# Spacer tensors that shift matmul operands by 32 or 96 bytes in one decoder layer

## What is computed

```python
for l in range(DEPTH):
    mix = hybrid_mixer(x, w_in[l], b_in[l], pool_w[l], ...)   # pooling, RG-LRU and short-conv branches, gates
    x = layer_norm(ALPHA * x + mix, ln_g[l, 0], ln_b[l, 0])
    xa = memory_cross_attention(x, mem, xa_w_q[l], xa_w_k[l], xa_w_v[l], xa_w_o[l])   # 4 heads, 256 memory tokens
    x = layer_norm(ALPHA * x + xa, ln_g[l, 1], ln_b[l, 1])
    ff = swiglu(x, ffn_w_gate[l], ffn_w_up[l], ffn_w_down[l])   # 1024 -> 2816 -> 1024
    x = layer_norm(ALPHA * x + ff, ln_g[l, 2], ln_b[l, 2])
```

## Time and profile before

| | |
|---|---|
| median of 3 executions | 1027.07 us (1026.95 to 1035.94) |
| the profiled execution's own time | 1027.04 us |
| its span, first to last instruction | 1025.3 us |
| TensorE busy | 1012.6 us (99%), 5740 matmuls |
| TensorE weight loads busy | 888.3 us (87%) |
| VectorE, ScalarE, GpSimd busy | 620.1, 442.9, 42.4 us |
| DMA | 110.88 MB, mean 108 GB/s |

### The profile page before, as it was taken

The page is one execution under the profiler, slowest core; times in us unless marked ns, Lnnn a source line. Parts: engine busy times, 40 slices in busy tenths (PEclk is TensorE's granted clock), DMA queues, the critical chain, the costliest instruction groups (busy, mean ns, idle before and its releaser), DMA issues.

```text
span 1025.3 us, 14409 instructions
## 1 busy us (share of the span) xinstructions
PE 1012.6 (99%) x5740; PEld 888.3 (87%) x5740; DVE 620.1 (60%) x818; ACT 442.9 (43%) x599; POOL 42.4 (4%) x36
## 2 busy tenths in 40 slices
PE   8999999999999999999999999999999999999997
PEld 8888888888888888888888998889999999988886
DVE  5768485876633333326585555488888888743336
ACT  5454646445422222223354434265654554532232
POOL 1000000000000000000040000040000000000000
PEclk9999999999999999999999999999999999999999
DMA  6324234132622323325253323204442432333212
GB/s 208 115 78 136 83 97 128 56 98 80 196 83 87 119 82 92 113 82 207 81 183 111 118 86 121 80 24 139 126 127 83 124 124 83 124 123 110 95 41 82
DMA packets 89040, 110.88 MB, mean 108 GB/s; under 512 B 2444, under 2 KB 81440, under 8 KB 88992
## 3 DMA queue, kind: packets, MB, share of 16 engines
q1 hardware_dynamic: 87024, 103.82, 31.9%
q0 software_dynamic: 1824, 6.32, 1.8%
q10 hardware_dynamic: 144, 0.05, 0.0%
HBM read 108.09 MB, written 2.10 MB: 107 GB/s over the span
## 4 chain that ended last, share of the span: by engine, by line
PE 95%; DVE 2%; ACT 1%; DMA 1%; POOL 0%; issue 0%; SPq 0%; DVEq 0%
PE ps L602 32%; PE ps L604 31%; PE ps L603 31%; DMA act<-in_x 1%; PE ps L631 1%; DVE xnat L1472 1%; DVE xT_l L1422 0%; ACT ps L1084 0%; PE ps L837 0%; POOL wl L565 0%; DVE probs L1463 0%; ACT wh L1042 0%; DVE wl L1414 0%; DVE xnat L1453 0%; ACT xa L1056 0%
## 5 line engine op out<-in xcount | busy, mean ns | idle before, releaser
L1414 DVE TENSOR_TENSOR wl<-raw,wh 128x1024 fp32r<-128x1024 f32 (+1 forms) x146 | 173.5, 1194 | 273.2 <-ACT wh L1042 271.7
L1042 ACT ACTIVATE wh<-raw 128x1024 fp32r<-128x1024 f32 x152 | 156.2, 1036 | 324.6 <-PE ps L604 304.0
L602 PE MATMUL ps<-xT_h,wh 128*128 128x512 f32 (+1 forms) x592 | 227.6, 384 | 1.3 <-DVE xT_l L1422 1.3
L604 PE MATMUL ps<-xT_h,wl 128*128 128x512 f32 (+1 forms) x592 | 226.9, 383 | 0.0
L603 PE MATMUL ps<-xT_l,wh 128*128 128x512 f32 (+1 forms) x592 | 226.9, 383 | 0.0
L602 PEld LDWEIGHTS ps<-xT_h,wh 128*128 128x128 f32 x592 | 111.3, 188 | 23.5 <-DVE xT_l L1422 1.5
L604 PEld LDWEIGHTS ps<-xT_h,wl 128*128 128x128 f32 x592 | 111.3, 188 | 21.8
L603 PEld LDWEIGHTS ps<-xT_l,wh 128*128 128x128 f32 x592 | 111.3, 188 | 21.7
L602 PE MATMUL ps<-wh,st_h 128*128 128x512 f32 x304 | 118.8, 391 | 0.0
L603 PE MATMUL ps<-wl,st_h 128*128 128x512 f32 x304 | 118.3, 389 | 0.0
L604 PE MATMUL ps<-wh,st_l 128*128 128x512 f32 x304 | 118.3, 389 | 0.0
(11 more groups left out here) (261 smaller groups left out, 1673.1 us busy)
## 6 DMA issues: line engine op xcount, KB each, us to landing
raw<-in_w_in SPq DMA_DIRECT2D x31, 1024.0 KB, 5.7
raw<-in_ffn_w_down SPq DMA_DIRECT2D x11, 1024.0 KB, 4.9
raw<-in_ffn_w_gate SPq DMA_DIRECT2D x20, 512.0 KB, 4.4
gb<-in_ffn_w_up SPq DMA_DIRECT2D x10, 512.0 KB, 4.2
raw<-in_ffn_w_up SPq DMA_DIRECT2D x10, 512.0 KB, 4.3
raw<-in_lru_w_out SPq DMA_DIRECT2D x4, 1024.0 KB, 5.0
raw<-in_sconv_w_out SPq DMA_DIRECT2D x4, 1024.0 KB, 5.8
raw<-in_w_mix_out SPq DMA_DIRECT2D x4, 1024.0 KB, 4.7
```

Of the source, the lines that this page charges most:

```text
L602: nc.tensor.matmul(dst, st, mv_, start=start, stop=False, skip_group_check=shared)
L604: return nc.tensor.matmul(dst, st_lo_part, mv_, start=False, stop=stop, skip_group_check=shared)
L1042: nc.scalar.activation(wh[:, ring(phase, s), 0:size], src, ACT.Copy).then_inc(w_hi.sem, 1)
L1414: nc.vector.tensor_tensor(wl[:, slot, 0:size], src, wh[:, slot, 0:size].bitcast(F32), ALU.subtract).then_inc(w_lo.sem, 1)
```

## The change

Six spacers are added, and three old ones grow, so that some operands start off a multiple of 256 bytes. No instruction is added, removed or moved: on every engine the same instructions stand in the same order, with other SBUF addresses.

```diff
--- before.py
+++ after.py
@@ -136,24 +136,28 @@
 
 
         with ExitStack() as scope:
+            sb("to_lru", [P, 8], F32, scope)
             lru_h = sb("lru_h", [P, KT, SEQ], F32R, scope)
             lru_l = sb("lru_l", [P, KT, SEQ], F32R, scope)
+            sb("to_cnv", [P, 16], F32, scope)
             cnv_h = sb("cnv_h", [P, KT, SEQ], F32R, scope)
             cnv_l = sb("cnv_l", [P, KT, SEQ], F32R, scope)
         with ExitStack() as scope:
 
 
-            sb("lru_first", [P, KT - 2, SEQ], F32, scope)
+            sb("lru_first", [P, (KT - 2) * SEQ + 8], F32, scope)
             u1 = sb("u1", [P, POOL_PAD + SEQ], F32, scope)
-            sb("to_cnv_h", [P, (2 * KT + KT - 2) * SEQ - (KT - 2) * SEQ - (POOL_PAD + SEQ)], F32, scope)
+            sb("to_cnv_h", [P, (2 * KT + KT - 2) * SEQ - (KT - 2) * SEQ - (POOL_PAD + SEQ) + 16], F32, scope)
             ra1 = sb("ra1", [P, 2, SEQ], F32, scope)
             sb("cnv_first", [P, KT - 2, SEQ], F32, scope)
             si1 = sb("si1", [P, 2, SEQ], F32, scope)
 
         with ExitStack() as scope:
             s1, s4, s2, s3 = (sb(name, [P, 1024], F32, scope) for name in ("s1", "s4", "s2", "s3"))
+        sb("to_st", [P, 8])
         st_h = sb("st_h", [P, SPLIT_SLOTS, SEQ], F32R)
         st_l = sb("st_l", [P, SPLIT_SLOTS, SEQ], F32R)
+        sb("past_st", [P, 56])
         gb = sb("gb", [P, 2, D])
         xnat = sb("xnat", [P, TT, D])
         with ExitStack() as scope:
@@ -172,8 +176,10 @@
         scaled = probs[:].rearrange("p t m -> p (t m)")
 
         with ExitStack() as scope:
+            sb("to_p", [P, 56], F32, scope)
             p_h = sb("p_h", [P, 2, SEQ], F32R, scope)
             p_l = sb("p_l", [P, 2, SEQ], F32R, scope)
+            sb("to_vr", [P, 48], F32, scope)
             vr_h = sb("vr_h", [P, 2, SEQ], F32R, scope)
             vr_l = sb("vr_l", [P, 2, SEQ], F32R, scope)
             u = (sb("u", [P, POOL_PAD + SEQ], F32, scope)[:], u1[:])
@@ -192,6 +198,7 @@
             memT_h = sb("memT_h", [P, KT, M], F32R, scope)
             memT_l = sb("memT_l", [P, KT, M], F32R, scope)
             mem_nat = sb("mem_nat", [P, MT, D], F32, scope)
+            sb("to_pT", [P, 40], F32, scope)
             pT_h = sb("pT_h", [P, MT, SEQ], F32R, scope)
             pT_l = sb("pT_l", [P, MT, SEQ], F32R, scope)
         with ExitStack() as scope:
@@ -202,7 +209,7 @@
             x12 = sb("x12", [P, 2, 4, 256], F32R, scope)
             xf = sb("xf", [P, 5, 4, 256], F32, scope)
         hidden = sb("hidden", [P, HT, SEQ])
-        sb("past_ig", [P, 32])
+        sb("past_ig", [P, 136])
         cur = sb("cur", [P, DECAY_EXP + 1, 2])
         soft = sb("soft", [P, 8, KT])
```

## The result

The changed kernel takes 1036.5 us (median of 18 executions) against 1027.01 us for the kernel before (18 executions on the same chips): 9.5 us more, a ratio of 1.0089 with a 95% interval of 1.0067 to 1.011. I had forecast 1017.8 us. What happened is the rival named "slower" in the form "settle one step higher", whose price was 1036.6 us.

The account below looks back on a forecast made before the run. TensorE, busy for 1012.6 of 1025.3 us, was taken as the bound. 1027.04 us less 9.60 (one 6.67 ns step on 1440 matmuls) plus 0.23 and 0.1 not reaching the end gave 1017.8 us; range 1011.5 to 1028.5 us.

Parts of the forecast that it names:

- the rival named "slower": Touched matmuls: shifted pairs don't settle, or settle higher; 1033.3 us at 231 ns, 1036.6 us at 233.3 ns; chance 0.11.
- settle one step higher: 1440 touched matmuls at 233.3 ns distance instead of 226.7: 9.6 us more, 1036.6 us; within a case of chance 0.11.
- What bounds the kernel: Whole kernel: TensorE busy 1012.6 of 1025.3 us, so time is matmul count times distance, plus a few small waits.
- N/2.4 plus a fixed overhead at difference 0: Matmuls with both operands on 0: 13.4 ns beyond 512 columns, 13.3 beyond 256, so overhead belongs to matmul, not column.
- Plus a second step where both operands stand at the same place: Each matmul pays another 6.67 ns if its operands coincide within 256 bytes; shifting 1440 touched ones saves 9.60 us.
- The row of 387 ns: A 512-column record behind a pause, a distance of 224 ns, taken to show that 226.7 ns is no floor.
- The first products of F: F's products on `xa`, 256 columns, displaced: 117.7 ns for some 2.8 us, called unsettled, 4.5 ns above the settled 113.2.
- The rival "more than one step": Touched matmuls: new shifts collide less than 192 does; at 215.8 ns, 15.2 us off, 1011.8 us; chance 0.14.
- The one-side rival: Shift helps only the moving operand (528 matmuls, 1023.5 us) or only the stationary one (912, 1021.3 us); chance 0.09.
- The rival "nothing": Touched 512-column matmuls stay at 226.7 ns, overhead perhaps one sixteenth of the columns; time stays 1027.0 us; chance 0.24.
- Cover and scratch tensors: Around the LayerNorms 0.23 and about 0.1 us of the saving is lost; moved scratch tensors on VectorE cost 0.
- Ports that never wait: TensorE's two independent SBUF read ports, by the skill: PE never waits, shifts are worth nothing, time stays 1027.0 us.

Follow-up runs that it names:

- the bare streams: Kernels without the layer, streaming only float32r matmuls at various operand starts and widths; 512 columns with equal starts settled at 226.7 ns, 32 bytes apart at 233.3 ns.

## Why the prediction was wrong, step by step

- **What bounds the kernel: right.** The sum over matmul distances is the time. 1440 matmuls moved by 6.4 to 6.7 ns each moved the kernel by 9.5 us; no wait appeared, and `xT`, `memT` and F kept their records as foreseen.
- **N/2.4 plus a fixed overhead at difference 0: right for four of five widths.** 320 and 384 columns, which no row of before had, came out at 146.7 and 173.3 ns, to the decimal. 448 did not (206.7 for 200.0), so it is no law.
- **"Plus a second step where both operands stand at the same place": this is the step that failed.** I had one displaced placement at one width, F's, and read its 113.2 ns as one step of a law without a width in it. F's shift does give F its 6.7 ns (11.9 us in the whole, with the shift taken away), but the same shift of 192 bytes at 512 columns costs 6.7 ns. The size was right, the sign was not, and the size by luck: the shifts used here are 32, 96, 160 and 224 bytes, and those cost 6.6 to 7.6 ns in the bare streams, where 64 bytes cost 2.2. Three numbers that fit a law are weak evidence where only one of them, at one width, carries the term in question.
- **The row of 387 ns: read for too much.** It showed that one 512-column matmul can pass in 224 ns. It didn't show that a stream can. In the bare streams single records of 388 ns do occur, at a start of 64 bytes, but in a cycle with 392 and 394, and the mean distance is 229. What had to be forecast was the mean of a settled stream.
- **The first products of F: a warning that I used only for the lower bound.** I called their 117.7 ns in the earlier trace rows unsettled. The bare streams show that it is a settled state of its own: it held to the end of groups of 48 and 72 matmuls, with the same addresses as the 113.3. That one placement has two paces in one trace already says that a shift doesn't fix the pace.
- **The slower rival: right in kind and price, too small in its chance.** "At 233.3 ns: 1440 x 6.67 = 9.6 us more, 1036.6 us" against 1036.5 measured. That its price fits so closely is again a matter of the shifts used. It got 0.11, because "F's products then do settle at 113.2 ns" was held against it, which again carried 256 columns over to 512. It should have had about as much as the forecast. The range ended at 1028.5 us and left this case out, although and the earlier trace rows showed slower paces at both widths.
- **The rival "more than one step": refuted where it was tried.** No stream of 512 columns settled below 226.7 ns at any start, pause or side. Its bound of 215.8 ns was weak from the outset: it set the 109 ns of a transpose beside 106.7, the time of 256 columns, but a transpose moves 128, and no row says how long those stream.
- **The one-side rival: the sides are alike.** The bare streams mirror each other, and in the layer the 528 moving-side and the 912 stationary-side matmuls cost nearly the same each (6.7 and 6.4 to 6.5 ns).
- **The rival "nothing", with its overhead of one sixteenth of the columns: refuted** by 320 and 384 columns.
- **Cover and scratch tensors: right as far as can be seen.** I had 0.3 of the 9.6 us not arriving. In the traces 9.2 us arrive between the first product and the last, and 9.5 by the medians, which is too close to tell. From the last `st` matmul to the end it is 7.0 us before and after, as foreseen. VectorE's total is 619.8 us against 620.1.
- **Ports that never wait** (the Trainium skill, SBUF — State Buffer, section "Who interferes with whom"): as the prediction said, the trace didn't agree for 256 columns, and it doesn't for 512 either: 389 against 395 ns with nothing but the start of one operand changed.

What stays open is the cause beneath the distances: why a shift helps at one width and hurts at another, and why 448 columns have the largest overhead at difference 0. The runs give the distances by start, width and entry; no run looks at the memory itself. The records of the weight loads (PEld) narrow it a little. Moving operand at 0, then at 32 with 512 columns:

```profile
L120 PEld LDWEIGHTS ps<-m_zero_h,w_h x24: 187/188/330, 22.3 to 39.6; 128*128 128x128 f32 x24
...
L124 PEld LDWEIGHTS ps<-m_thirtytwo_h,w_h x24: 187/187/188, 57.0 to 73.1; 128*128 128x128 f32 x24
```

The load takes 187 to 188 ns at either start, so the 6.7 ns don't show in it. With 256 columns it is a little longer at difference 0 (median 192 ns) than with the stationary operand at 192 (187 to 188). Nor was how far the tensors lie from each other beyond their remainders varied, other than by 256 and 512 bytes.

## What to carry to other kernels

Where an address sets a matmul's pace, measure it at the width that is used, and as a settled stream: a start that gains 6.7 ns with 256 columns loses 6.7 ns with 512. With float32r products of 512 columns let both operands start at the same place within 256 bytes; that is also the placement that needs no spacer. A short stream of matmuls alone, one source line for each placement, gives these paces in one run of 0.4 ms, and its numbers held in the layer within 0.6 ns (233.8 for 233.3, 229.5 for 228.9, 117.8 for 117.8). Where a placement has two paces, as F's has, one stream doesn't show it; that takes several entries.

## What the runs showed of the hardware that was not expected

- At the full clock the distance of float32r matmuls depends on the difference of the two starts within 256 bytes, for 512 columns: 226.7 ns at 0, 228.8 to 236.7 ns at all eleven others tried (8, 16, 32, 48, 64, 96, 128, 160, 192, 224, 240). Shifting both operands alike, by 32 or by 192, changes nothing (226.7).
- With 256 columns a difference of 192 has two settled states, 113.4 and 117.8 ns, and one of 16 has three, 113.4, 118.7 and 120.0; what comes ahead of the stream (its pause or its first PSUM bank) decides. In the layer the slower state of F was worth 7.2 us in the one profile that shows it; it would be 1872 x 4.4 = 8 us with all of F in it.
- Many settled distances are multiples of 6.67 ns: 113.3, 120.0, 146.7, 173.3, 200.0, 206.7, 226.7, 233.3. Most are means over a few unequal steps, and not all fit: 116.7, 117.8 and 229.0 do not.
